# Who adds up the weight tiles of a seven-product gate matrix: GpSimd instead of VectorE

## The chip, the cores and the metric

The kernel runs on one core of one Trainium2 chip. The metric is the device time in microseconds (us) of one execution. The kernel before took 2365.54 us, the median of three runs (2364.66 to 2366.19). One more execution was recorded by the hardware profiler; all rows below are from it.

Engines are named as in the profile: PE is the matrix engine (PEld its loading of weights), DVE is VectorE, ACT is ScalarE, POOL is GpSimd, SP only issues transfers here. SBUF is the on-chip memory, a bank is an accumulator of PE.

## The reference

Two transformer layers over 512 positions of 1024 features, in float32: the first with two SwiGLU blocks around a mixer, the second with a mixer, a memory attention and a third SwiGLU block. What matters here is a SwiGLU block; there are three of them, of hidden width 2816.

```python
def swiglu_ffn(h, w_in, w_out):
    a, b = jnp.split(h @ w_in, 2, axis=-1)
    return (jax.nn.silu(a) * b) @ w_out

def _swiglu(h, w_gate, w_up, w_down):
    return (jax.nn.silu(h @ w_gate) * (h @ w_up)) @ w_down
```

## The kernel before, in words

All matrix products are made of float32 operands that are split in two parts, `hi` and `lo`, each of which PE takes whole: a product is `hi*hi + hi*lo + lo*hi`, three matmuls. Activations are split once and kept; weights are streamed. A *unit* is one weight tile of 128 rows and up to 1024 columns. It goes through four hands: SP issues its load into one of four `raw` buffers, ACT writes `whi` (one of three buffers; L1747), DVE writes `raw - whi` over the raw data as `wlo` (L2206), and PE multiplies. A `raw` buffer is loaded again when PE is through with the unit of four before, and `whi` is written again when PE is through with the unit of three before.

All engines walk through the same list of work items; each program is written out in this order, and within an engine nothing overtakes. Before the item that uses unit u, ACT and DVE put the splits of the units up to u+2.

In the second and third SwiGLU block most products with the gate matrix are not made directly. Two neighbouring tiles of 128 gate columns and two blocks of 128 rows form a 2 by 2 block matrix, whose product with a 2 by 2 block of the activations takes seven block products in place of eight (a Strassen scheme in Winograd's form). The sums of the activations are made once. The sums of the weights are made for each unit: it is loaded with four tiles of 128x128, and four more are added up from them in place, so that the unit is 1024 columns wide again. This is `add_up`: one instruction for two tiles (L2340) and one each for the other two (L2343, L2345), of which each needs the one before. ACT may split the unit only when the last sum is there (the semaphore `w_sum`). There are 60 such units in 15 *rounds*. A round makes two gate tiles and the two tiles of the other matrix that belong to them:

- unit q0 (seven block products, 21 matmuls of 256 columns), then b (a plain unit, 24 matmuls of 512 columns), q1
- `ffg` of the odd tile of the round before: DVE takes its bank (L2334), multiplies (L2396), ACT copies, DVE writes the low half (L2211)
- `ffv`: DVE takes b's bank (L2334, `t_bt`)
- q2, q3, then `ffm`: ACT copies out a quarter (`t_p`), DVE joins the seven products by six instructions on the banks (L2366 to L2373) and two more (L2377)
- b2 (plain), and `ffg` of the even tile

The rounds use six banks: four for q0 to q3, one each for b and b2. The next round's q0 takes the same four, and so waits until the last of the six instructions (L2373) has read them.

The rounds stand in four stretches: 3 and 5 rounds in the second block (from 1122 to 1191 us and from 1258 to 1354 us of the span), 2 and 5 in the third (2058 to 2104 and 2172 to 2267 us). In a stretch a prime marks the units of the next round: q0', b' and so on.

In DVE's program the sums stand between the splits: as far as the unit after the one just split, and up to three units ahead of the item:

```python
while n < min(upto - 1 + NHI, len(unit)):
    while a < min(n + 1 + (n in summands), upto + NHI, len(unit)):
        if a in summands:
            add_up(a)
        a += 1
    split(n)
    n += 1
```

Of the kernel before, what the change touches and what calls it, by code (L numbers as in the profile page):

```python
# [10 lines left out]
ALU = mybir.AluOpType  # L11
# [3 lines left out]
P = 128  # L15
# [72 lines left out]
NHI = 3  # L88
WARM = 6
NRAW = 4  # L90
# [889 lines left out]
def build(nc, A, out):  # L980
    stack = ExitStack()
    w = order()
    unit = w.units
# [12 lines left out]
    def place(name, at, cols, dt=F32):  # L996

        assert at + cols <= ARENA + NRAW * UNIT
        return nc.alloc_sbuf_tensor_at("t_" + name, [P, cols], dt, offset=base + 4 * at)[:]

    def f32(ap):
        return ap.bitcast(F32)

    raw = [place(f"raw{i}", ARENA + i * UNIT, UNIT) for i in range(NRAW)]
# [109 lines left out]
    def spare(hd, t):  # L1114

        return (pp2 if hd.kind in ("win", "mm2") else pp)[t % RING]
# [10 lines left out]
    def width(hd, i):  # L1127
        if hd.kind == "spa":
            return (i + 1) * P
        return P if hd.kind == "win" and i == 0 else 256  # L1130
# [11 lines left out]
    def signal(name):  # L1142
        return Signal(stack.enter_context(nc.semaphore("s_" + name)))

    full = signal("bank_full")
    w_hi, w_lo, w_sum, x_full = signal("weight_hi"), signal("weight_lo"), signal("weight_sum"), signal("operand_full")
# [4 lines left out]
    d_raw = [signal(f"d_raw{i}") for i in range(NRAW)]  # L1151
# [16 lines left out]
    def squares(what, h, q):  # L1168
        if what == "k":
            return T[h][:, 256 * q:256 * q + 256]  # L1170
        return T[q] if h else T[2 + q]
# [1018 lines left out]
    summands = set(w.seven)  # L2190

    def dve_program(e):
        on = Once(e)
# [3 lines left out]
        def split(n):  # L2197
            name, _, width, _ = unit[n]
            width = UNIT if n in summands else width
            on.wait_ge(*w_hi.at(n))  # L2200
            if name in STACKED:
                m, at = STACKED[name]
                x, hi = (t.rearrange("p (k c) -> p k c", k=KD) for t in (raw[n % NRAW], whi[n % NHI]))
                e.tensor_tensor(hi[:, :, at:at + m], x[:, :, 0:m], f32(hi[:, :, 0:m]), ALU.subtract).then_inc(*w_lo.tick(n))
                return
            e.tensor_tensor(wlo[n % NRAW][:, 0:width], raw[n % NRAW][:, 0:width], f32(whi[n % NHI][:, 0:width]),  # L2206
                            ALU.subtract).then_inc(*w_lo.tick(n))
# [125 lines left out]
            on.wait_ge(*full.at(item))  # L2333
            e.tensor_tensor(o, banks[item], RB, ALU.mult).then_inc(*evac.tick(done, ("free", item)))  # L2334

        def add_up(n):
            r = raw[n % NRAW]
            on.wait_ge(*d_raw[n % NRAW].at(n))
            two = r[:, 512:768].rearrange("p (a c) -> p a c", a=2)
            e.tensor_tensor(two, r[:, 128:384].rearrange("p (a c) -> p a c", a=2), r[:, 384:512].unsqueeze(1).to_broadcast([P, 2, P]),  # L2340
                            ALU.add).then_inc(*w_sum.tick(("two", n)))
            on.wait_ge(*w_sum.at(("two", n)))
            e.tensor_tensor(r[:, 768:896], r[:, 640:768], r[:, 128:256], ALU.add).then_inc(*w_sum.tick(("three", n)))  # L2343
            on.wait_ge(*w_sum.at(("three", n)))
            e.tensor_tensor(r[:, 896:1024], r[:, 768:896], r[:, 0:128], ALU.add).then_inc(*w_sum.tick(n))  # L2345

        def xna(f, j):
            b, a = TN[j % 2]
            x = NS[j]
            on.wait_ge(*x_full.at(("xn", f, j)))  # L2350
            e.tensor_tensor(x[:, 0:256], b[:, 256:512], b[:, 0:256], ALU.subtract).then_inc(*calc.tick(("xn1", f, j)))
            e.tensor_tensor(x[:, 256:512], b[:, 256:512], a[:, 256:512], ALU.subtract).then_inc(*calc.tick(("xn3", f, j)))
            on.wait_ge(*calc.at(("xn1", f, j)))
            e.tensor_tensor(x[:, 512:768], a[:, 256:512], x[:, 0:256], ALU.subtract).then_inc(*calc.tick(("xn2", f, j)))
            on.wait_ge(*calc.at(("xn2", f, j)))
            e.tensor_tensor(x[:, 768:1024], a[:, 0:256], x[:, 512:768], ALU.subtract).then_inc(*calc.tick(("xns", f, j)))
# [544 lines left out]
        def final(k):  # L2901
            n = 2 if k < 6 else 1
            if k == 7:
# [13 lines left out]
                  winzero=winzero, kaz=kaz, vaf=vaf, vas=vas, qa=qa, oasum=oasum, oa=oa, om=om, alr=alr, gq=gq, gkv=gkv, gdec=gdec, gone=gone, glog=glog, gcum=gcum, ggate=ggate,  # L2917
                  gkt=gkt, gstate=gstate, gg=gg, gsq=gsq, gnorm=gnorm, gfin=gfin, osplit=osplit, mk2s=mk2s, mk2d=mk2d,
                  mem2zero=mem2zero, mv2s=mv2s, mq2x=mq2x, mq2s=mq2s, mmo=mmo, final=final)
        n, a = 2, 2  # L2920
        for (kind, *args), upto in w.items:
            while n < min(upto - 1 + NHI, len(unit)):
                while a < min(n + 1 + (n in summands), upto + NHI, len(unit)):
                    if a in summands:
                        add_up(a)
                    a += 1
                split(n)
                n += 1
            while a < min(upto + NHI, len(unit)):
                if a in summands:  # L2930
                    add_up(a)
                a += 1
            if kind in do:
                do[kind](*args)

    def pool_program(e):
        on = Once(e)

        def scale(t):
            hd, i = w.tiles[t]  # L2940
            wd = width(hd, i)
            p, r = spare(hd, t)[:, 0:wd], sa[t % RING][:, 4:5]
            on.wait_ge(*calc.at(("rc", t)))
            if hd.kind == "spa":
                on.wait_ge(*calc.at(("gn",)))
                k = 3 * (4 * hd.more["g"] + hd.more["r"]) + 1 + hd.more["a"]
                e.tensor_scalar(p, p, r, gn[:, i, k:k + 1], ALU.mult, ALU.mult).then_inc(*scaled.tick(t))  # L2947
            else:
                on.wait_ge(*d_c.at(0))
                e.tensor_scalar(p, p, r, cst[:, C_ONE:C_ONE + 1], ALU.mult, ALU.mult).then_inc(*scaled.tick(t))  # L2950

        def widestat(what, h):
            a, b = squares(what, h, 0), squares(what, h, 1)
            on.wait_ge(*curve.at(("wsq", what, h, 1)))
            e.tensor_tensor(a, a, b, ALU.add).then_inc(*summed.tick(("wsq", what, h)))

        def winload():
            on.wait_ge(*full.at(("ffo", 1, 0, 0)))
            e.memset(lrw, 0.0).then_inc(*cleared.tick("lrw"))

        def hidzero():
            on.wait_ge(*full.at(("memv", 1, 1)))
            for q in range(2):
                e.memset(hk[2 * q], 0.0)
                e.memset(hk[2 * q + 1], 0.0).then_inc(*cleared.tick("hid"))

        def cclear(g):
            on.wait_ge(*full.at(("values", 3 + 8 * g)))
            for q in range(2):
                e.memset(f32(PCT[q]), 0.0).then_inc(*cleared.tick(("kcp", g)))  # L2970

        def final(k):
            if k == 7:
                on.wait_ge(*curve.at(("gain", 7)))
                on.wait_ge(*copied.at(("rb", 6)))
                e.tensor_tensor(XT[:, 7, :], XT[:, 7, :], RB, ALU.mult).then_inc(*scaled.tick(("final", 7)))

        do = dict(widestat=widestat, winload=winload, final=final, cclear=cclear, scale=scale, hidzero=hidzero)
        for (kind, *args), _ in w.items:
            if kind in do:  # L2980
                do[kind](*args)

# [89 lines left out]
    for program in (pe_program, act_program, dve_program, pool_program, sp_program):  # L3072
        program(Count())
# [3 lines left out]
    block.tensor(pe_program)  # L3077
    block.scalar(act_program)
    block.vector(dve_program)
    block.gpsimd(pool_program)  # L3080
    block.sync(sp_program)
    stack.close()
# [80 lines left out]
```

## Time and profile before

| | |
|---|---|
| median of three runs | 2365.54 us |
| the profiled execution | 2364.08 us |
| its span, first to last instruction | 2362.3 us |
| clock granted to PE | 0.999 of full speed |
| PE busy | 2338.0 us (99%) |
| DVE busy | 1559.0 us (66%) |
| ACT busy | 1051.7 us (45%) |
| POOL busy | 165.5 us (7%) |
| DMA, mean over the span | 98 GB/s |

A matmul's record is longer than its share of the engine: matmuls are pipelined, and of 512 columns one starts every 0.227 us though each is shown with 0.39 us, of 256 columns one every 0.120 us with 0.28 us. PE's small stops are therefore read from the distance of starts. A row of a timeline gives start, duration, engine, line, operation, tiles and shapes, the count of merged instructions, and in brackets the idle time before it and what ended it. The chain that ended last runs over PE for 96% of the span.

### The profile page before, as it was taken

To read this page: it belongs to the slowest core of one execution; us is meant where nothing else is said; L and a number is where in the kernel's file an instruction comes from. 1 tells how busy PE (TensorE), PEld (TensorE's weight loads), DVE (VectorE), ACT (ScalarE), POOL (GpSimd) and SP (SyncE) were. 2 spreads that over 40 slices of the span, in tenths; PEclk is the share of its full clock that TensorE was granted. 3 is DMA by queue.
4 is the path that set the end of the run, shared out by engine and by line. 5 is a ranking of instruction groups with operands and counts; after the bars stand their busy time and mean duration, and the time that the engine had idled before them with its cause. 6 is when DMAs were issued, how large, how long until landed. Compare 5 with 4: busy or idle time off the path is not lost.

```text
span 2362.3 us, 31755 instructions
## 1 busy us (share of the span) xinstructions
PE 2338.0 (99%) x11988; PEld 1980.8 (84%) x11988; DVE 1559.0 (66%) x3231; ACT 1051.7 (45%) x1921; POOL 165.5 (7%) x250
## 2 busy tenths in 40 slices
PE   9999999999999999999999999999999999999998
PEld 7888889888888888878888888888888887888887
DVE  6434546674757897877756856677754667774864
ACT  4323335432335676664333434666523346432432
POOL 0000000110001222310000000111100001000000
PEclk9999999999999999999999999999999999999999
DMA  4454434332322211122233333211123332233232
GB/s 151 118 117 144 118 109 153 111 109 84 116 94 86 77 54 63 59 92 96 90 104 103 98 117 120 81 54 55 63 89 114 123 112 72 90 97 95 94 106 90
DMA packets 98416, 231.42 MB, mean 98 GB/s; under 512 B 8984, under 2 KB 39320, under 8 KB 98266
## 3 DMA queue, kind: packets, MB, share of 16 engines
q1 hardware_dynamic: 93072, 221.42, 28.3%
q10 hardware_dynamic: 5194, 7.98, 2.1%
q8 instruction: 97, 1.59, 0.3%
q14 instruction: 53, 0.43, 0.1%
HBM read 217.83 MB, written 11.53 MB: 97 GB/s over the span
## 4 chain that ended last, share of the span: by engine, by line
PE 96%; DVE 2%; ACT 1%; issue 1%; DMA 0%; POOL 0%; DVEq 0%; SPq 0%; ACTq 0%
PE bank L1186 93%; PE bank L1453 2%; PE bank L1261 1%; PE bank L1627 0%; PE bank L1282 0%; DVE t_pw L2532 0%; DMA t_XT<-in_xT 0%; DVE t_pp L2532 0%; DVE t_PS L2211 0%; DVE t_wlo L2206 0%; DVE t_XL L2215 0%; ACT t_whi L1747 0%; ACT t_pw L1917 0%; DVE t_XT L2908 0%; POOL t_pw L2950 0%
## 5 line engine op out<-in xcount | busy, mean ns | idle before, releaser
L1186 PE MATMUL bank<-t_XH,t_whi 128*128 128x512 f32 (+1 forms) x2004 | 770.4, 384 | 1.2 <-DVE t_wlo L2206 0.5
L1186 PE MATMUL bank<-t_XL,t_whi 128*128 128x512 f32 (+1 forms) x2004 | 761.6, 380 | 0.0
L1186 PE MATMUL bank<-t_XH,t_wlo 128*128 128x512 f32 (+1 forms) x1988 | 755.5, 380 | 0.0
L2206 DVE TENSOR_TENSOR t_wlo<-t_raw,t_whi 128x1024 fp32r<-128x1024 f32 (+2 forms) x446 | 514.2, 1156 | 322.3 <-ACT t_whi L1747 318.5
L1747 ACT ACTIVATE t_whi<-t_raw 128x1024 fp32r<-128x1024 f32 (+3 forms) x452 | 448.3, 993 | 427.4 <-PE bank L1186 320.0
L1186 PEld LDWEIGHTS bank<-t_XH,t_whi 128*128 128x128 f32 x2004 | 377.1, 188 | 75.6 <-DVE t_tmp L2373 2.6
L1186 PEld LDWEIGHTS bank<-t_XH,t_wlo 128*128 128x128 f32 x1988 | 373.8, 188 | 72.0
L1186 PEld LDWEIGHTS bank<-t_XL,t_whi 128*128 128x128 f32 x2004 | 377.4, 188 | 67.5
L1186 PE MATMUL bank<-t_RX,t_whi 128*128 128x512 f32 x1056 | 325.2, 389 | 0.0
L1186 PEld LDWEIGHTS bank<-t_RX,t_whi 128*128 128x128 f32 x1056 | 198.3, 188 | 40.9
L1186 PE MATMUL bank<-t_RX,t_wlo 128*128 128x512 f32 x528 | 205.4, 389 | 0.0
L2334 DVE TENSOR_TENSOR t_tmp<-bank,t_RB 128x512 f32<-128x512 f32 x133 | 91.6, 689 | 104.3 <-PE bank L1186 95.5
L1186 PEld LDWEIGHTS bank<-t_RX,t_wlo 128*128 128x128 f32 x528 | 99.1, 188 | 20.7
L2947 POOL TENSOR_SCALAR t_pp<-t_pp,t_sa,t_gn 128x512 f32<-128x512 f32 (+3 forms) x128 | 88.7, 699 | 334.9 <-DVE t_sa L2545 334.4
L1747 ACT ACTIVATE t_RX<-t_tmp 128x512 fp32r<-128x512 f32 x66 | 41.7, 632 | 156.9 <-DVE t_tmp L2396 156.9
L1917 ACT ACTIVATE t_pp<-t_pp,t_sa 128x256 f32<-128x256 f32 (+3 forms) x144 | 79.6, 554 | 53.1 <-DVE t_sa L2532 52.3
L2950 POOL TENSOR_SCALAR t_pw<-t_pw,t_sa,t_cst 128x256 f32<-128x256 f32 (+1 forms) x80 | 47.9, 604 | 722.2 <-DVE t_sa L2545 692.8
L1852 ACT ACTIVATE t_tmp<-t_tmp 128x512 f32<-128x512 f32 x66 | 41.5, 629 | 126.8 <-DVE t_tmp L2334 85.8
L1747 ACT ACTIVATE t_XH<-t_XT,t_vec 128x512 fp32r<-128x512 f32 x48 | 34.5, 723 | 109.2 <-DVE t_XT L2409 52.6
L1186 PE MATMUL bank<-t_OA,t_whi 128*128 128x512 f32 x256 | 79.4, 391 | 0.0
L2409 DVE SCALAR_TENSOR_TENSOR t_XT<-bank,t_XT 128x512 f32<-128x512 f32 x47 | 32.5, 691 | 68.6 <-PE bank L1186 68.6
L2211 DVE TENSOR_TENSOR t_RX<-t_tmp,t_RX 128x512 fp32r<-128x512 f32 x66 | 45.8, 693 | 46.0 <-ACT t_RX L1747 46.0
(360 smaller groups left out, 3197.5 us busy)
## 6 DMA issues: line engine op xcount, KB each, us to landing
t_raw<-in_f_in SPq DMA_DIRECT2D x70, 512.0 KB, 3.2
t_raw<-in_f_out SPq DMA_DIRECT2D x32, 384.0 KB, 3.1
t_raw<-in_w_conv SPq DMA_DIRECT2D x24, 512.0 KB, 3.2
t_raw<-in_w_merge SPq DMA_DIRECT2D x24, 512.0 KB, 3.2
t_raw<-in_fu SPq DMA_DIRECT2D x22, 512.0 KB, 3.2
t_raw<-in_f_out SPq DMA_DIRECT2D x32, 320.0 KB, 2.9
t_raw<-in_f_in SPq DMA_DIRECT2D x36, 256.0 KB, 2.8
t_raw<-in_w_g SPq DMA_DIRECT2D x16, 512.0 KB, 3.2
```

The source lines that it names most:

```text
L1186: return e.matmul(o, l, r, start=start, stop=stop, skip_group_check=True)
L1261: f = e.transpose(b[:, i * P:(i + 1) * P], r, ident)
L1453: f = e.transpose(b[:, j * P:(j + 1) * P], spare(hd, t)[:, j * P:(j + 1) * P], ident)
L1747: return e.activation(o, i, ACT.Copy, **how)
L1852: e.activation(s, a, ACT.Silu).then_inc(*curve.tick(("silu", f, h, m)))
L1917: e.activation(p, p, ACT.Exp, scale=-1.0, bias=s[:, 0:1], accum_out=s[:, 1:2]).then_inc(*curve.tick(("ex", t)))
L2206: e.tensor_tensor(wlo[n % NRAW][:, 0:width], raw[n % NRAW][:, 0:width], f32(whi[n % NHI][:, 0:width]), ALU.subtract).then_inc(*w_lo.tick(n))
L2211: e.tensor_tensor(o, x, f32(hi), ALU.subtract).then_inc(*x_lo.tick(item, *more))
L2334: e.tensor_tensor(o, banks[item], RB, ALU.mult).then_inc(*evac.tick(done, ("free", item)))
L2409: e.scalar_tensor_tensor(XT[:, m, :], banks[item], HALF[f], XT[:, m, :], ALU.mult, ALU.add).then_inc(*evac.tick(("free", item), *done))
L2947: e.tensor_scalar(p, p, r, gn[:, i, k:k + 1], ALU.mult, ALU.mult).then_inc(*scaled.tick(t))
L2950: e.tensor_scalar(p, p, r, cst[:, C_ONE:C_ONE + 1], ALU.mult, ALU.mult).then_inc(*scaled.tick(t))
```

## The change

`add_up` moves from DVE's program into POOL's, as it stands. DVE's loop keeps only the splits. POOL's loop, which so far took only items of its own, puts before each item the sums of units up to three beyond the item's own (`upto + NHI`). The waits are the same: on the unit's load, on the sum before, and ACT's on `w_sum`.

```diff
@@ dve_program
-        def add_up(n):
-            r = raw[n % NRAW]
-            on.wait_ge(*d_raw[n % NRAW].at(n))
-            two = r[:, 512:768].rearrange("p (a c) -> p a c", a=2)
-            e.tensor_tensor(two, r[:, 128:384].rearrange("p (a c) -> p a c", a=2), r[:, 384:512].unsqueeze(1).to_broadcast([P, 2, P]),
-                            ALU.add).then_inc(*w_sum.tick(("two", n)))
-            on.wait_ge(*w_sum.at(("two", n)))
-            e.tensor_tensor(r[:, 768:896], r[:, 640:768], r[:, 128:256], ALU.add).then_inc(*w_sum.tick(("three", n)))
-            on.wait_ge(*w_sum.at(("three", n)))
-            e.tensor_tensor(r[:, 896:1024], r[:, 768:896], r[:, 0:128], ALU.add).then_inc(*w_sum.tick(n))
...
-        n, a = 2, 2
+        n = 2
         for (kind, *args), upto in w.items:
             while n < min(upto - 1 + NHI, len(unit)):
-                while a < min(n + 1 + (n in summands), upto + NHI, len(unit)):
-                    if a in summands:
-                        add_up(a)
-                    a += 1
                 split(n)
                 n += 1
-            while a < min(upto + NHI, len(unit)):
-                if a in summands:
-                    add_up(a)
-                a += 1
             if kind in do:
                 do[kind](*args)
@@ pool_program
+        def add_up(n):
...
         do = dict(widestat=widestat, winload=winload, final=final, cclear=cclear, scale=scale, hidzero=hidzero)
-        for (kind, *args), _ in w.items:
+        n = 2
+        for (kind, *args), upto in w.items:
+            while n < min(upto + NHI, len(unit)):
+                if n in summands:
+                    add_up(n)
+                n += 1
             if kind in do:
                 do[kind](*args)
```

On DVE, from `ffv` of one round to `ffm`: before, the sum of q0' (three rows on `t_raw`) stands between the splits of b2 and of q0'.

```order
L2334 TENSOR_TENSOR t_bt_182<-bank,t_RB 128x512 [waits s_bank_full]
L2206 TENSOR_TENSOR t_wlo_55<-t_raw_51,t_whi 128x1024 [waits s_weight_hi]
L2340 TENSOR_TENSOR t_raw_52<-t_raw_52 128x256 [waits s_d_raw3]
L2343 TENSOR_TENSOR t_raw_52<-t_raw_52 128x128 [waits s_weight_sum]
L2345 TENSOR_TENSOR t_raw_52<-t_raw_52 128x128 [waits s_weight_sum]
L2206 TENSOR_TENSOR t_wlo_56<-t_raw_52,t_whi 128x1024 [waits s_weight_hi]
L2366 TENSOR_TENSOR t_p_185<-bank,t_p_184 128x256 [waits s_bank_copied]
```

And now, at the same place (line numbers from here on are smaller by 11 in the changed kernel):

```order
L2334 TENSOR_TENSOR t_bt_182<-bank,t_RB 128x512 [waits s_bank_full]
L2206 TENSOR_TENSOR t_wlo_55<-t_raw_51,t_whi 128x1024 [waits s_weight_hi]
L2206 TENSOR_TENSOR t_wlo_56<-t_raw_52,t_whi 128x1024 [waits s_weight_hi]
L2355 TENSOR_TENSOR t_p_185<-bank,t_p_184 128x256 [waits s_bank_copied]
```

The three rows are gone; the two splits and `ffm` follow each other. The other three sums of a round go in the same way: that of q1' from ahead of L2396, those of q2' and q3' from around the split of q1'.

On POOL, in the same round: before, nothing stands there (the memset of `t_lrw`, whose wait ends between the first two stretches, is followed by work of the second mixer). Now:

```order
L2963 TENSOR_TENSOR t_raw_52<-t_raw_52 128x256 [waits s_d_raw3]
L2966 TENSOR_TENSOR t_raw_52<-t_raw_52 128x128 [waits s_weight_sum]
L2968 TENSOR_TENSOR t_raw_52<-t_raw_52 128x128 [waits s_weight_sum]
L2963 TENSOR_TENSOR t_raw_50<-t_raw_50 128x256 [waits s_d_raw1]
L2966 TENSOR_TENSOR t_raw_50<-t_raw_50 128x128 [waits s_weight_sum]
L2968 TENSOR_TENSOR t_raw_50<-t_raw_50 128x128 [waits s_weight_sum]
```

These are the sums of q0' (buffer 52) and q1' (buffer 50), one unit after another, with no other wait than that for the load and for the sum before.

## Rows read from the trace of the kernel before

**Rows 1.** The page, busy time of each engine, share of the span, instructions.

```profile
PE 2338.0 (99%) x11988; PEld 1980.8 (84%) x11988; DVE 1559.0 (66%) x3231; ACT 1051.7 (45%) x1921; POOL 165.5 (7%) x250
```

**Rows 2.** Busy time in the four stretches of rounds, summed (us; x instructions).

```profile
sum 306.00, PE 305.74 PEld 273.53 DVE 242.45 ACT 120.89 POOL 0.00; mean PE 76.44 PEld 68.38 DVE 60.61 ACT 30.22 POOL 0.00
```

**Rows 3.** Timeline of PE where a round begins, in four rounds; 1332.58 is q1'.

```profile
1180.01 0.39 PE L1186 MATMUL bank<-t_XH,t_wlo 128*128 128x512 f32 x1
1180.33 0.36 PE L1186 MATMUL bank<-t_XH,t_whi 128*128 128x256 f32 x1
...
1324.19 0.39 PE L1186 MATMUL bank<-t_XH,t_wlo 128*128 128x512 f32 x1
1324.52 0.36 PE L1186 MATMUL bank<-t_XH,t_whi 128*128 128x256 f32 x1
...
1332.58 0.28 PE L1186 MATMUL bank<-t_XH,t_whi 128*128 128x256 f32 x1
...
2213.49 0.39 PE L1186 MATMUL bank<-t_XH,t_wlo 128*128 128x512 f32 x1
2214.14 0.36 PE L1186 MATMUL bank<-t_XH,t_whi 128*128 128x256 f32 x1 [0.26 <-issue]
...
2256.16 0.39 PE L1186 MATMUL bank<-t_XH,t_wlo 128*128 128x512 f32 x1
2256.48 0.36 PE L1186 MATMUL bank<-t_XH,t_whi 128*128 128x256 f32 x1
```

**Rows 4.** Timeline of DVE, one round of the second stretch.

```profile
1317.22 1.22 DVE L2206 TENSOR_TENSOR t_wlo<-t_raw,t_whi 128x1024 fp32r<-128x1024 f32 x1
1318.35 0.42 DVE L2340 TENSOR_TENSOR t_raw<-t_raw 128x256 f32<-128x256 f32 x1
...
1320.55 1.23 DVE L2206 TENSOR_TENSOR t_wlo<-t_raw,t_whi 128x1024 fp32r<-128x1024 f32 x1 [1.13 <-ACT t_whi L1747]
...
1323.48 0.68 DVE L2373 TENSOR_TENSOR t_tmp<-bank,t_p 128x512 f32<-128x512 f32 x1
...
1338.39 1.22 DVE L2206 TENSOR_TENSOR t_wlo<-t_raw,t_whi 128x1024 fp32r<-128x1024 f32 x1
```

**Rows 5.** Timeline of ACT, the same round.

```profile
1319.45 1.06 ACT L1747 ACTIVATE t_whi<-t_raw 128x1024 fp32r<-128x1024 f32 x1 [2.53 <-DVE t_raw L2345]
...
1332.83 1.06 ACT L1747 ACTIVATE t_whi<-t_raw 128x1024 fp32r<-128x1024 f32 x1 [1.28 <-PE bank L1186]
```

**Rows 6.** Timeline of SP's issues, the same round.

```profile
1314.11 0.37 SPq L2997 DMA_DIRECT2D t_raw<-in_f_in  x1
...
1319.15 8.52 SPq L2997 DMA_DIRECT2D t_raw<-in_f_in  x3
```

**Rows 7.** The 60 loads of such units (L2997): issue to landing.

```profile
DMA to landing us min/median/max: 2.5/2.7/4.0
```

**Rows 8.** Groups on POOL by shape: count | busy us, mean ns | idle before, releasers.

```profile
L2955 POOL TENSOR_TENSOR t_tmp<-t_tmp 128x512 f32<-128x512 f32 x4 | 5.2, 1294 | 18.7 <-ACT t_tmp L1880 18.7
L2955 POOL TENSOR_TENSOR t_tmp<-t_tmp 128x256 f32<-128x256 f32 x4 | 3.0, 744 | 383.6 <-ACT t_tmp L1880 383.6
L2950 POOL TENSOR_SCALAR t_pw<-t_pw,t_sa,t_cst 128x128 f32<-128x128 f32 x16 | 7.3, 458 | 307.9 <-DVE t_sa L2545 301.1 <-DVE t_sa L2542 6.8
```

**Rows 9.** POOL's L2950 of 128x256: count, ns min/median/max, first and last start.

```profile
L2950 POOL TENSOR_SCALAR t_pp<-t_pp,t_sa,t_cst x16: 557/560/2501, 417.6 to 602.1; 128x256 f32<-128x256 f32 x16
```

**Rows 10.** Timeline of POOL at two places where DVE splits weights.

```profile
453.57 1.28 POOL L2955 TENSOR_TENSOR t_tmp<-t_tmp 128x512 f32<-128x512 f32 x1
...
495.03 2.50 POOL L2950 TENSOR_SCALAR t_pp<-t_pp,t_sa,t_cst 128x256 f32<-128x256 f32 x1 [9.33 <-DVE t_sa L2545]
```

**Rows 11.** Timeline of DVE at the same two places.

```profile
453.73 3.33 DVE L2206 TENSOR_TENSOR t_wlo<-t_raw,t_whi 128x1024 fp32r<-128x1024 f32 x2 [0.47 <-ACT t_whi L1747]
...
494.77 0.15 DVE L2545 RECIPROCAL t_sa<-t_sa 128x1 f32<-128x1 f32 x1
494.84 2.34 DVE L2206 TENSOR_TENSOR t_wlo<-t_raw,t_whi 128x1024 fp32r<-128x1024 f32 x2
```

More of the change, by code:

```diff
@@ L2976, in final @@
                 e.tensor_tensor(XT[:, 7, :], XT[:, 7, :], RB, ALU.mult).then_inc(*scaled.tick(("final", 7)))
-        do = dict(widestat=widestat, winload=winload, final=final, cclear=cclear, scale=scale, hidzero=hidzero)
-        for (kind, *args), _ in w.items:
+        def add_up(n):
+            r = raw[n % NRAW]
+            on.wait_ge(*d_raw[n % NRAW].at(n))
+            two = r[:, 512:768].rearrange("p (a c) -> p a c", a=2)
+            e.tensor_tensor(two, r[:, 128:384].rearrange("p (a c) -> p a c", a=2), r[:, 384:512].unsqueeze(1).to_broadcast([P, 2, P]),
+                            ALU.add).then_inc(*w_sum.tick(("two", n)))
+            on.wait_ge(*w_sum.at(("two", n)))
+            e.tensor_tensor(r[:, 768:896], r[:, 640:768], r[:, 128:256], ALU.add).then_inc(*w_sum.tick(("three", n)))
+            on.wait_ge(*w_sum.at(("three", n)))
+            e.tensor_tensor(r[:, 896:1024], r[:, 768:896], r[:, 0:128], ALU.add).then_inc(*w_sum.tick(n))
+        do = dict(widestat=widestat, winload=winload, final=final, cclear=cclear, scale=scale, hidzero=hidzero)
+        n = 2
[4 more added lines that the diff above has]
+                n += 1
             if kind in do:
```

## The prediction

> **What bounds the kernel now.** I read the page first. PE is busy for 2338.0 of 2362.3 us [rows 1], so a gain is at most what PE's stops hold, and a loss is whatever makes PE stop. The change touches only the four stretches of rounds, so I read these next: summed over them, PE is busy 305.74 of 306.00 us, DVE 242.45, ACT 120.89 and POOL 0.00 [rows 2]. DVE is at work four fifths of the time, but nobody there waits for DVE as a whole; what counts is which wait on its chain ends last.
>
> The busy time hides PE's small stops, since a matmul's record overlaps the next one's. By the distance of starts there is one where a round's q0 begins: after the last matmul of b2, at 1324.19, the next starts 0.33 us later, where 0.227 is usual, and is itself shown with 0.36 in place of 0.28 us, so some 0.17 to 0.18 us are lost [rows 3]. I find this at seven of the 15 q0, the first at 1180.33 and the last at 2256.48; six are of this size, the one at 2214.14 is 0.65 − 0.23 + 0.07, about 0.5 us [rows 3]. In all 6 × 0.17 + 0.5 = 1.5 us. Elsewhere in the stretches no start is late by 0.1 us.
>
> What ends that stop is the bank: the last instruction of `ffm` on the banks, L2373, starts at 1323.48 and takes 0.68, to 1324.16, and q0's first matmul follows 0.36 later at 1324.52 [rows 3, 4]. Behind it stands a chain on DVE and ACT: split of b2 at 1317.22, sum of q0' from 1318.35, ACT's split of q0' at 1319.45, DVE's at 1320.55, then `ffm` [rows 4, 5]. So in the later rounds of a stretch the sum is on the chain that PE waits for, and 0.1 us more there is 0.1 us more of PE. The next tight place is b2: its split ends 1338.39 + 1.22 = 1339.61; with the 0.36 us from write to matmul that is 1339.97. PE goes on from b' at 1332.58 with three q units of 21 × 0.12 = 2.52 us and wants b2 near 1340.1: 0.15 us of slack [rows 3, 4].
>
> **The change part by part.** Taken from DVE: 60 sums. The first instruction is 0.42 us, and from its start at 1318.35 to ACT's at 1319.45 a whole sum is 1.1 us [rows 4, 5]. That is 66 us less of DVE and by itself nothing for PE, except where the sum stands on the chain above.
>
> Added to POOL: 60 × 3 instructions. POOL's add of two SBUF tiles takes 0.744 us for 256 columns and 1.294 for 512 [rows 8], 2.15 ns a column; for 128 columns I estimate 0.744 − 128 × 2.15 ns = 0.47. A tensor_scalar of 128 columns, 0.458 [rows 8], is the lower bound, the 256-column add, 0.744, the upper. The first instruction reads one operand three-dimensionally, once broadcast, which no row shows on POOL: bounds 0.744 and, for twice the columns, 1.294; I take 0.744, the same column count. From a DVE result to POOL's start 0.11 us pass (494.77 + 0.15 to 495.03) [rows 10, 11]; I take 0.1 for each of the two inner waits. A free sum is then 0.744 + 2 × 0.47 + 0.2 = 1.9 us, 0.8 more than on DVE (by the upper bounds 1.294 + 2 × 0.744 + 0.2 = 3.0). In return it need not stand in DVE's row: it starts when the load lands. The order of loads and splits, and PE's program, are unchanged; no new DMA, and the only new wait is POOL's for the load, behind which nothing but other sums is queued in these stretches.
>
> The sums are not free, though. POOL's add of 453.57 (1.28 us, to 454.85) runs beside two splits of DVE that take 3.33 us in place of 2.34 [rows 10, 11]: the first is held until POOL is done and ends about 1.1 us later. In the other direction a 0.56 us instruction of POOL takes 2.50 us at 495.03, until two splits that stand back to back (494.84 to 497.18) are over [rows 9, 10, 11]. So a DVE instruction with two SBUF inputs and an instruction of POOL exclude each other, and DVE's back-to-back instructions keep POOL out. The Trainium skill has the first half of this (SBUF — State Buffer, section Who interferes with whom): a VectorE instruction with two SBUF inputs contends with a GpSimd instruction that reads SBUF, one fully blocks. The trace agrees, with 3.33 us against 2.34. Were it otherwise, the sums would run freely and the result would be the first rival below; with it, the splits, L2396, L2377 and L2211 of DVE all stand against the sums.
>
> Now one round, placed by hand. *Place A, the sum of q0'.* Issue 1314.11, landing 2.7 us later at 1316.8 [rows 6, 7], some 1.5 us before DVE took it up. POOL's first instruction runs 1316.9 to 1317.65. DVE's split of b2, ready at 1317.22, is held and ends near 1318.75 in place of 1318.44: 0.3 late. POOL's second instruction is held in turn by this split, and runs to about 1319.15, the third to 1319.7; ACT starts near 1319.75 in place of 1319.45. So the early start is lost in full, and the chain to the banks is 0.3 us later. *Place B, the sums of q2' and q3'.* The last of the three loads is issued at 1319.15 + 8.52 − 0.37 = 1327.30 [rows 6] and lands at 1330.0. POOL has q2' in hand from 1327.4 on: 1.9 us, and in the way L2211 (0.69) and the split of q1' (1.22), so it comes to 1330.5 to 1331.2. Then q3': 1.9 us and the split of q2' (1.13), to 1333.5 to 1334.2, where ACT took it at 1332.83 as soon as PE let it [rows 5]. That is 0.7 to 1.4 late if every collision happens. But DVE's instructions there come up to 2 us earlier (three sums have left its row), so that some fall ahead of a landing; I take 0 to 0.5. What is late here reaches b2, through L2334, L2396, ACT's copy and the split at 1338.39, where 0.15 us are free.
>
> A and B lie on one chain through the round. I take 0.3 us a round: place A in full, place B hidden by the earlier row on DVE. Bounds: −0.17 (no collision, the stop goes) and +0.8 (0.3 + 0.5). There are 15 − 4 = 11 passages from one round to the next within a stretch: 11 × 0.3 = 3.3 us. I count the four that have no stop now like the others, since the chain is within a few tenths there. The profiled execution took 2364.08 us, 1.8 of it outside the span; it would take 2367.4. The median of the runs stands 1.5 above it, at 2365.54, and goes to 2368.8 us. What a measurement of this kernel can tell from no change is about 0.2%, 4.7 us: below 2360.8 or above 2370.3.
>
> **The rivals.** *The stops vanish.* If the sums fall mostly between DVE's instructions, the chain gets 1.1 us shorter and PE's 1.5 us are gained: 2364.0. For it: POOL is idle in all four stretches, loads land 1.5 us ahead. Against: the split of b2 is ready 0.3 us after POOL's first start, in every round. It can't be faster by more, since PE has no other stops there.
>
> *The collisions add up (slower).* Place B decides: if the sum of q3' is ready over 0.5 us after PE frees ACT's buffer, b2's split is late as well and each round loses 0.8: 11 × 0.8 = 8.8 us, 2374.3. For it: POOL kept out for 2.50 us by back-to-back splits [rows 10]. Against: between the splits of q1' and q2' DVE waits for ACT.
>
> *POOL's adds are dear.* With the upper bounds a sum is 1.1 us longer, q2' and q3' stand behind each other, so 2.2 + 0.3 us a round, 11 × 2.5 = 27 us, 2393. Against: only the broadcast form is unknown.
>
> That the change doesn't do what it says is excluded by the order: the three rows are gone from DVE and stand on POOL.
>
> **How the numbers follow.** Forecast 0.50, stops vanish 0.22, collisions add up 0.20, dear adds 0.08. Forecast's own range 2365.5 to 2372 (0 to 0.6 a round); about a sixth of it, 0.08, is above 2370.3. Slower: 0.08 + 0.20 + 0.08 = 0.36; faster 0.02, for something unseen; same 0.62. The range 2363.5 to 2377 holds the first rival, the forecast and the second rival (with 1.0 a round), and leaves out the dear adds and the tails.
>
> **What would show it.** Right: POOL's three instructions at some 0.75, 0.47 and 0.47 us where nothing is in the way, longer where a split runs; splits of up to 1.9 us on DVE; PE's stop ahead of q0 at 0.4 to 0.5 us rather than 0.17, and hardly one ahead of b2. DVE about 60 us less busy, POOL 100 us or more busier. Wrong: no stop at q0 (the first rival), stops ahead of b2 in each round (the second), or POOL's first instruction at over 1 us with DVE idle beside it (the third).

## The result and the profile after

| | before | after |
|---|---|---|
| median of the runs | 2364.91 us (2363.36 to 2366.54, 22 runs) | 2368.72 us (2366.54 to 2370.46, 22 runs) |
| ratio after : before | | 1.0015, 95% interval 1.0009 to 1.0021 |
| the profiled execution | 2364.08 us | 2368.48 us |
| its span | 2362.3 us | 2366.6 us |

The changed kernel is slower by 3.8 us of 2365 (2.1 to 5.0 by the interval): a loss, though one of less than the 0.2% within which I had called it no change.

The page, busy time of each engine after:

```profile
PE 2340.9 (99%) x11988; PEld 1983.5 (84%) x11988; DVE 1510.2 (64%) x3051; ACT 1050.6 (44%) x1921; POOL 303.3 (13%) x430
```

Against [rows 1], 180 instructions went from DVE to POOL. DVE lost 48.8 us of busy time, POOL got 137.8. The three groups of the new instructions, by shape (count | busy us, mean ns of one | idle before, and what ended it):

```profile
L2963 POOL TENSOR_TENSOR t_raw<-t_raw 128x256 f32<-128x256 f32 x60 | 49.2, 820 | 442.8 <-DMA t_raw<-in_f_in 226.6 <-DMA t_raw<-in_fg 216.1
...
L2968 POOL TENSOR_TENSOR t_raw<-t_raw 128x128 f32<-128x128 f32 x60 | 48.5, 809 | 4.7
L2966 POOL TENSOR_TENSOR t_raw<-t_raw 128x128 f32<-128x128 f32 x60 | 41.6, 694 | 4.7
```

In all 139.3 us. What one of them takes with nothing in its way, and what with a split of DVE in its way, is read in the timeline. POOL, one round (the same round of the program as in [rows 3 to 6], some 2.3 us later on the clock); the first three rows are the sum of q0', then q1', q2' and q3':

```profile
1319.11 0.73 POOL L2963 TENSOR_TENSOR t_raw<-t_raw 128x256 f32<-128x256 f32 x1 [5.30 <-DMA t_raw<-in_f_in]
1319.93 1.32 POOL L2966 TENSOR_TENSOR t_raw<-t_raw 128x128 f32<-128x128 f32 x1
1321.32 0.46 POOL L2968 TENSOR_TENSOR t_raw<-t_raw 128x128 f32<-128x128 f32 x1
1323.97 0.76 POOL L2963 TENSOR_TENSOR t_raw<-t_raw 128x256 f32<-128x256 f32 x1 [2.19 <-DMA t_raw<-in_f_in]
1324.81 0.47 POOL L2966 TENSOR_TENSOR t_raw<-t_raw 128x128 f32<-128x128 f32 x1
1325.35 0.46 POOL L2968 TENSOR_TENSOR t_raw<-t_raw 128x128 f32<-128x128 f32 x1
1329.70 0.74 POOL L2963 TENSOR_TENSOR t_raw<-t_raw 128x256 f32<-128x256 f32 x1 [3.89 <-DMA t_raw<-in_f_in]
1330.52 0.79 POOL L2966 TENSOR_TENSOR t_raw<-t_raw 128x128 f32<-128x128 f32 x1
1331.39 1.32 POOL L2968 TENSOR_TENSOR t_raw<-t_raw 128x128 f32<-128x128 f32 x1
1332.68 0.74 POOL L2963 TENSOR_TENSOR t_raw<-t_raw 128x256 f32<-128x256 f32 x1
1333.50 0.46 POOL L2966 TENSOR_TENSOR t_raw<-t_raw 128x128 f32<-128x128 f32 x1
1334.04 1.35 POOL L2968 TENSOR_TENSOR t_raw<-t_raw 128x128 f32<-128x128 f32 x1
```

DVE in the same round: the split of b2, the split of q0', the release of the banks (the old L2373), the splits of q1' and q2', and the split of b2':

```profile
1319.40 1.53 DVE L2206 TENSOR_TENSOR t_wlo<-t_raw,t_whi 128x1024 fp32r<-128x1024 f32 x1
1322.91 1.23 DVE L2206 TENSOR_TENSOR t_wlo<-t_raw,t_whi 128x1024 fp32r<-128x1024 f32 x1 [1.98 <-ACT t_whi L1747]
...
1325.84 0.68 DVE L2362 TENSOR_TENSOR t_tmp<-bank,t_p 128x512 f32<-128x512 f32 x1
...
1331.11 1.29 DVE L2206 TENSOR_TENSOR t_wlo<-t_raw,t_whi 128x1024 fp32r<-128x1024 f32 x1
1333.84 1.22 DVE L2206 TENSOR_TENSOR t_wlo<-t_raw,t_whi 128x1024 fp32r<-128x1024 f32 x1 [1.44 <-ACT t_whi L1747]
...
1340.97 1.22 DVE L2206 TENSOR_TENSOR t_wlo<-t_raw,t_whi 128x1024 fp32r<-128x1024 f32 x1
```

The two lists are to be read side by side. Free adds (q1') take 0.76, 0.47 and 0.46 us. Where a split stands in the way, an add takes 1.3 us and ends just after the split: 1319.93 + 1.32 = 1321.25 beside the split that ends at 1320.93, and so at 1331.39 and 1334.04. In the other direction the split of b2 takes 1.53 instead of 1.22, since POOL's first add runs until 1319.84. Over all, POOL pays more: 139.3 us against 60 × (0.74 + 0.47 + 0.46) = 100, so 39 us of holding. DVE lost 48.8 us of busy time, though its sums took 60 (60 × (0.42 + 0.29 + 0.29)); most of the difference is that a sum's record overlaps the one before it (1318.35 lies ahead of 1317.22 + 1.22 in [rows 4]). What DVE was held for is read from its groups with two SBUF inputs: the splits took 431.2 us in place of 428.9, the low halves of `ffg` (L2211) 46.9 in place of 45.8, the two multiplications of `ffm` (L2377) 19.9 in place of 19.2, some 4 us in all.

Where it comes back to PE. ACT's waits in the second stretch, 1258 to 1366 us (what waited <- for what: us in total, times, longest), first before:

```profile
ACT t_whi L1747 <- DVE t_raw L2345: 18.3, 10, 2.8
...
ACT t_whi L1747 <- PE bank L1186: 11.9, 6, 3.0
```

and after:

```profile
ACT t_whi L1747 <- POOL t_raw L2968: 34.7, 15, 4.3
...
ACT t_whi L1747 <- PE bank L1186: 2.0, 1, 2.0
```

Before, six of ACT's splits in this stretch started as soon as PE freed the buffer; after, one. The others now wait for POOL's last add. PE's own rows, after, at a b2, at a q0 and at the last b2 of the second stretch (start, duration):

```profile
1320.86 0.28 PE L1186 MATMUL bank<-t_XH,t_wlo 128*128 128x256 f32 x1
1321.08 0.47 PE L1186 MATMUL bank<-t_XH,t_whi 128*128 128x512 f32 x1
...
1326.37 0.39 PE L1186 MATMUL bank<-t_XH,t_wlo 128*128 128x512 f32 x1
1326.88 0.36 PE L1186 MATMUL bank<-t_XH,t_whi 128*128 128x256 f32 x1
...
1363.63 0.28 PE L1186 MATMUL bank<-t_XH,t_wlo 128*128 128x256 f32 x1
1364.89 0.47 PE L1186 MATMUL bank<-t_XH,t_whi 128*128 128x512 f32 x1 [0.98 <-DVE t_wlo L2206]
```

A stop is read as for [rows 3]: the distance of starts above 0.12 or 0.227 us, plus what the next distance has too much (0.07 to 0.08). At 1321.08 it is 0.17 us, at 1326.88 0.36, at 1364.89 1.22. POOL and DVE ahead of the last of these three:

```profile
1352.41 1.79 POOL L2963 TENSOR_TENSOR t_raw<-t_raw 128x256 f32<-128x256 f32 x1 [4.92 <-DMA t_raw<-in_f_in]
```

```profile
1352.38 1.23 DVE L2206 TENSOR_TENSOR t_wlo<-t_raw,t_whi 128x1024 fp32r<-128x1024 f32 x1 [0.26 <-ACT t_whi L1747]
```

I added up all stops in the rounds, by place, for every kernel that was run (the last b2 of a stretch, which lies behind the windows of [rows 2], is counted with it). The kernels with e are the experiments below; each difference is to the kernel before of the same series, 2364.80 us for e1, e2, e3 and e4, 2365.76 us for the others:

| kernel | stops ahead of q0, us (count) | ahead of b2, us (count) | together, less before | measured: difference of medians, us; ratio (95%) |
|---|---|---|---|---|
| before | 1.51 (7) | 0.15 (1) | | |
| after | 2.18 (7) | 2.62 (6) | +3.1 | +3.8; 1.0015 (1.0009 to 1.0021) |
| e1_writes | 0 | 0 | −1.7 | −0.7; 0.9995 (0.9986 to 1.0004) |
| e2_q0_dve | 3.10 (7) | 2.62 (5) | +4.1 | +4.9; 1.0019 (1.0011 to 1.0028) |
| e3_q0_pool | 2.82 (8) | 0.62 (4) | +1.8 | +2.7; 1.0011 (1.0003 to 1.0020) |
| e3b_q1_pool | 1.65 (7) | 0 | 0.0 | −0.3; 0.9998 (0.9989 to 1.0007) |
| e4_fourth | 5.72 (8) | 11.43 (11) | +15.5 | +17.6; 1.0069 (1.0056 to 1.0083) |
| e5_beside | 3.31 (7), and 0.78 (3) ahead of q1 | 2.37 (5) | +4.8 | +5.9; 1.0025 (1.0016 to 1.0034) |
| e6b_after_early | 0 | 2.14 (9) | +0.5 | +0.8; 1.0003 (0.9994 to 1.0011) |
| e7b_before_early | 0 | 0 | −1.7 | −1.6; 0.9993 (0.9985 to 1.0002) |

The two columns at the right agree to about 1 us, less than the interval of a ratio leaves open (0.0009 is 2 us); for e4, of five runs only, to 2.1 us where the interval leaves 3. So PE's stops at these places carry the result, and of the 3.1 us lost by the change 2.47 (2.62 − 0.15) stand ahead of b2 and 0.67 ahead of q0. Where a stop stands is not yet what made it: e2 and e3 below show that each place makes stops at the other, too.

### The profile page after: what moved, and what is told of

The parts are those of the page before. It is cut to its first block, busy times and chain, and to the rows that moved or that the text cites. A ratio compares the mean times of both kernels' runs of the same rounds, so it can differ in the third digit from the quotient of the medians.

```text
span 2366.6 us, 31755 instructions
## 1 busy us (share of the span) xinstructions
PE 2340.9 (99%) x11988; PEld 1983.5 (84%) x11988; DVE 1510.2 (64%) x3051; ACT 1050.6 (44%) x1921; POOL 303.3 (13%) x430
## 4 chain that ended last, share of the span: by engine, by line
PE 95%; DVE 2%; ACT 1%; issue 1%; DMA 1%; POOL 0%; SPq 0%; DVEq 0%; ACTq 0%
PE bank L1186 91%; PE bank L1453 2%; PE bank L1261 1%; DVE t_wlo L2206 0%; PE bank L1627 0%; ACT t_whi L1747 0%; PE bank L1282 0%; DMA t_XT<-in_xT 0%; DVE t_pw L2521 0%; DMA t_raw<-in_f_in 0%; DVE t_PS L2211 0%; DMA t_raw<-in_fg 0%; POOL t_raw L2963 0%; ACT t_pw L1917 0%; DVE t_XT L2897 0%
## 5 line engine op out<-in xcount | busy, mean ns | idle before, releaser
L2963 POOL TENSOR_TENSOR t_raw<-t_raw 128x256 f32<-128x256 f32 x60 | 49.2, 820 | 442.8 <-DMA t_raw<-in_f_in 226.6
```

## The experiments

The theory: a POOL add that reads SBUF and a DVE instruction with two SBUF inputs exclude each other; the loss is made where a sum meets a split on the chain to PE (place A, the sum of q0'; place B, those of q2' and q3').

**Reads or writes.** Rival: GpSimd is slow to start and to signal, and the longer sum by itself is the loss.

```diff
...
+            e.memset(r[:, 512:1024], 0.0).then_inc(*w_sum.tick(("two", n)))
             on.wait_ge(*w_sum.at(("two", n)))
-            e.tensor_tensor(r[:, 768:896], r[:, 640:768], r[:, 128:256], ALU.add).then_inc(*w_sum.tick(("three", n)))
+            e.memset(r[:, 512:1024], 0.0).then_inc(*w_sum.tick(("three", n)))
...
```

> The changed kernel with GpSimd's three adds replaced by three memsets of 512 columns each at the same place and with the same waits (the sums are left out, the output is not the reference's). A memset reads nothing from SBUF; three take about as long as the three adds do alone (3 x 0.53 = 1.6 us against 1.7). Theory (VectorE's instructions with two SBUF inputs and GpSimd's reads exclude each other): no split is held and no memset is stretched, the unit is ready about 1.9 us after its load lands, which is earlier than VectorE's sum was; the stops of PE ahead of q0 (0.36 us in the changed kernel, 0.17 before) and of b2 go, so 1.5 us less than before, ratio 0.9993. Rival (GpSimd is late because its instructions and semaphores are slow, whatever VectorE does): stops as in the changed kernel, ratio 1.0015.

POOL in the same round, a unit that DVE's split of b2 meets; then that split:

```profile
1318.78 0.53 POOL L2962 MEMSET t_raw<- 128x512 f32 x1 [6.15 <-DMA t_raw<-in_f_in]
1319.36 0.53 POOL L2964 MEMSET t_raw<- 128x512 f32 x1
1319.94 0.52 POOL L2966 MEMSET t_raw<- 128x512 f32 x1
```

```profile
1319.21 1.21 DVE L2206 TENSOR_TENSOR t_wlo<-t_raw,t_whi 128x1024 fp32r<-128x1024 f32 x1
```

The split lies over three instructions of POOL and takes its 1.21 us; POOL's take theirs. So it is in all rounds: no memset takes over 0.53 us, no split over 1.23. The unit is ready 1.68 us after POOL's start, and ACT's split of q0', which waits for POOL's last memset as it waits for the last add in the changed kernel, starts at 1320.50, 1.29 us after the split of b2 began, where it was 2.23 us before [rows 4, 5]; the 0.2 us that a free sum takes longer would fit in. Every stop of PE in the rounds is gone. So neither POOL's signals nor its slower work cost PE anything: what costs is that POOL reads SBUF beside DVE. The rival falls.

**Place B without place A.** Only the sum of q0' goes back to DVE; q1' to q3' stay on POOL. (In e2, e3 and e3b the sums stand in both programs, and a set says which units of a round POOL adds up; they differ in this set alone.)

```diff
+    on_pool = {n for n in w.seven if unit[n][1][1] in (1, 2, 3)}
```

> The sums of q0 back on VectorE, those of q1, q2, q3 on GpSimd. Theory, place A (the sum of q0 is on the chain to the banks, 0.3 us a round): the stop ahead of q0 returns to about 0.17 us; what is left is the lateness of q2 and q3 (0.17 us ahead of b2 in some rounds), so 0 to +1.5 us, ratio 1.0000 to 1.0006. Rival (place B, the pair q2 and q3, makes the loss): stops ahead of both as in the changed kernel, ratio 1.0013 or more.

Here my theory that place A makes the loss fell: 1.0019, not less than the changed kernel. ACT's splits of q2' and q3' wait for POOL, and b2 is late:

```profile
1334.25 1.06 ACT L1748 ACTIVATE t_whi<-t_raw 128x1024 fp32r<-128x1024 f32 x1 [2.35 <-POOL t_raw L2989]
1336.92 1.06 ACT L1748 ACTIVATE t_whi<-t_raw 128x1024 fp32r<-128x1024 f32 x1 [1.61 <-POOL t_raw L2989]
```

The stops ahead of q0 double to 3.10 us although the sum of q0' stands on DVE again. DVE's split of b2 and its release of the banks:

```profile
1320.41 1.21 DVE L2208 TENSOR_TENSOR t_wlo<-t_raw,t_whi 128x1024 fp32r<-128x1024 f32 x1
...
1326.67 0.68 DVE L2375 TENSOR_TENSOR t_tmp<-bank,t_p 128x512 f32<-128x512 f32 x1
```

The chain to the banks is as long as before: from the split of b2 at 1320.41 to the end of the release at 1327.35 it is 6.94 us, as from 1317.22 to 1324.16 [rows 4]. But it begins with b2's split, and that is now late. Lateness made at B is paid at b2 and again at the next q0.

**Place A alone.**

```diff
+    on_pool = {n for n in w.seven if unit[n][1][1] in (0,)}
```

> Only the sums of q0 on GpSimd, the others on VectorE as before. Theory, place A: q0's second add is held by the split of b2, the stop ahead of q0 grows to about 0.36 us in the later rounds of each stretch, no stop ahead of b2; +2 us, ratio 1.0008 (1.0004 to 1.0013). Rival (place B makes the loss): as before, ratio 1.0000.

1.0011, which fits a cost at place A: it costs too. The four stops ahead of b2 (0.62 us) I had not expected: at three of them DVE's split of b2 is itself held by POOL's first add and takes 1.65 to 1.70 us. Both places are real, and they don't add up: +1.8 and +4.1 us of stops alone, +3.1 together. With q0' on POOL as well, its sum doesn't wait behind the late split of b2; that this returns a part of what B costs is my reading, which no run tests by itself.

**A sum that meets nothing.** q1' was the one that POOL made freely in the round above.

```diff
+    on_pool = {n for n in w.seven if unit[n][1][1] in (1,)}
```

> The kernel before with the sum of q1' alone on GpSimd, the one of the four that ran on GpSimd without being held. Theory (a sum costs where it meets a split on the chain; q1' has over 2 us before ScalarE wants it): ratio 1.0000, 0.9996 to 1.0004, stops as in the kernel before (0.17 ahead of q0, none ahead of b2). Rival (any sum on GpSimd costs by its length): 1.0005 and more, with new stops.

POOL in the same round:

```profile
1321.90 0.74 POOL L2984 TENSOR_TENSOR t_raw<-t_raw 128x256 f32<-128x256 f32 x1 [19.31 <-DMA t_raw<-in_f_in]
1322.71 0.46 POOL L2987 TENSOR_TENSOR t_raw<-t_raw 128x128 f32<-128x128 f32 x1
1323.26 0.46 POOL L2989 TENSOR_TENSOR t_raw<-t_raw 128x128 f32<-128x128 f32 x1
```

While POOL reads here, DVE is at `ffm` (from 1321.59 on), which takes one operand from a bank, and neither holds the other. No loss and no gain, 0.9998; PE's stop ahead of q0 is 0.17 us in most rounds, as before.

**More of the same.** The last add of each sum made twice on POOL.

```diff
+            e.tensor_tensor(r[:, 896:1024], r[:, 768:896], r[:, 0:128], ALU.add).then_inc(*w_sum.tick(("four", n)))
+            on.wait_ge(*w_sum.at(("four", n)))
```

> The changed kernel with the last sum made twice by GpSimd (same values), a fourth dependent instruction per unit. Theory (the sums are on the chain that PE waits for, and each dependent add gives VectorE one more turn): 0.55 us more for q0 and 0.55 to 1.7 more for q2 and q3 together, so stops ahead of q0 of 0.8 to 1 us or stops ahead of b2 as well; +0.6 to +1.2 us in each of 11 passages over the changed kernel, ratio to before 1.0043 to 1.007. Rival (the sums have slack, the loss comes from elsewhere, such as VectorE being held): ratio as in the changed kernel, 1.0015 to 1.002.

1.0069: one more add of 0.46 us a sum, and the loss grows more than fourfold, with two thirds of the stops ahead of b2 (11.43 of 17.2 us). The rival, that the sums have slack, falls; each add lengthens the chain and is one more that can be held. The stops at the two places explain 15.5 of the 17.6 us; the rest is within the interval, 3 us on either side.

**Holding without waiting.** The kernel before, and in the third block alone POOL adds constants beside the sums that DVE makes; nobody waits for them.

```diff
+        def beside(n):
...
+            on.wait_ge(*d_raw[n % NRAW].at(n))
...
+            e.tensor_tensor(scr, cst[:, 0:256], cst[:, 0:256], ALU.add).then_inc(*w_psum.tick(("two", n)))
...
+            e.tensor_tensor(scr[:, 0:128], cst[:, 0:128], cst[:, 128:256], ALU.add).then_inc(*w_psum.tick(("three", n)))
...
+            e.tensor_tensor(scr[:, 0:128], cst[:, 0:128], cst[:, 128:256], ALU.add).then_inc(*w_psum.tick(("last", n)))
```

> The kernel before, VectorE makes all sums; in the rounds of the third block alone (7 of 15, 5 passages) GpSimd makes three adds of the same sizes from constants into a scratch tile whenever such a unit has landed, and nobody waits for them. Theory (GpSimd's adds cost by holding VectorE's instructions with two SBUF inputs): the split of b2 or the sum of q0' is held by 0.3 to 0.8 us at each passage, so 5 x 0.3 to 0.8 = 1.5 to 4 us, ratio 1.0006 to 1.0017, in the trace larger stops ahead of q0 or b2 in stretches 3 and 4 alone, splits of 1.5 us and more there, and the stops of stretches 1 and 2 as in the kernel before. Rival (the cost comes from ScalarE waiting for GpSimd's slower sums, and the holding is small): 1.0000, 0.9996 to 1.0003, stops of stretches 3 and 4 as before.

1.0025, above the range of my theory, and in the other direction from the rival. POOL in one of these rounds, then DVE's sum of q0' beside it, then PE at that q0:

```profile
2232.64 1.49 POOL L2988 TENSOR_TENSOR t_scr<-t_cst 128x128 f32<-128x128 f32 x1
2234.21 0.52 POOL L2990 TENSOR_TENSOR t_scr<-t_cst 128x128 f32<-128x128 f32 x1
```

```profile
2233.74 0.68 DVE L2342 TENSOR_TENSOR t_raw<-t_raw 128x256 f32<-128x256 f32 x1
2234.45 0.43 DVE L2345 TENSOR_TENSOR t_raw<-t_raw 128x128 f32<-128x128 f32 x1
2234.92 0.29 DVE L2347 TENSOR_TENSOR t_raw<-t_raw 128x128 f32<-128x128 f32 x1
```

```profile
2239.27 0.39 PE L1188 MATMUL bank<-t_XH,t_wlo 128*128 128x512 f32 x1
2240.31 0.35 PE L1188 MATMUL bank<-t_XH,t_whi 128*128 128x256 f32 x1 [0.65 <-DVE t_tmp L2375]
```

DVE's own sum takes 0.4 us longer (0.68 and 0.43 in place of 0.42 and 0.29), and with b2 late by the same cause the stop at q0 becomes 0.89 us (1.04 − 0.23 + 0.08). The stops in the first two stretches are as before, four of 0.17. I had looked for long splits; only three of the 1024-column splits in the rounds took over 1.3 us, and what was held are mostly DVE's sums, which take 12.0 us more in all (29.4, 21.9 and 20.9 us by line in place of 25.2, 17.5 and 17.5). No instruction waits for POOL here, so holding alone is enough. A round loses more than in the changed kernel; I take it that this is because DVE is held and still has its sums to make.

**Another order, with and without the change.** The copy and the six bank instructions of `ffm` go ahead of the split of q0' on ACT and DVE; the two multiplications, `ffr` in the diff, stay behind it. The changed bound of the loop keeps the split of q0' from being put one item earlier.

```diff
         for (kind, *args), upto in w.items:
-            while n < min(upto - 1 + NHI, len(unit)):
+            if kind == "ffm":
+                do[kind](*args)
+            while n < min(upto - 1 + NHI - (kind == "ffs" and args[3] == 3), len(unit)):
...
+            if kind == "ffm":
+                ffr(*args)
+            elif kind in do:
                 do[kind](*args)
```

> The kernel before, with the copy and the six bank instructions of ffm put ahead of the split of q0' on ScalarE and VectorE (the two multiplications of ffm stay behind it). The banks are then free about 2 us earlier (near 1322.1 in place of 1324.16), and q0's split ends near 1323.3. Theory (the chain to the banks ends PE's stop ahead of q0): the seven stops are gone, 1.5 us less, ratio 0.9994, 0.9989 to 1.0000. Rival (q0's weights are then as late as the banks were): stops of some 0.2 us stay, 1.0000, 0.9997 to 1.0004.

> The changed kernel with the same two groups exchanged. Theory (place A acts through the release of the banks, place B, the sums of q2' and q3' kept out by VectorE's splits, through b2's split): the stops ahead of q0 are gone, those ahead of b2 (0.15 to 0.4) stay, so some 2 us of loss stay of 3.8: ratio 1.0004 to 1.0010. Rival 1 (all of it is place A's lateness handed on along the round): b2's stops go too, ratio 0.9994 to 1.0002. Rival 2 (the q0' chain ends at the weights, not at the banks): stops ahead of q0 stay, ratio 1.0015 as the changed kernel.

The kernel before in this order, DVE's release of the banks and the split of q0' behind it, then PE at q0:

```profile
1322.00 0.68 DVE L2375 TENSOR_TENSOR t_tmp<-bank,t_p 128x512 f32<-128x512 f32 x1
1322.60 1.21 DVE L2208 TENSOR_TENSOR t_wlo<-t_raw,t_whi 128x1024 fp32r<-128x1024 f32 x1
```

```profile
1324.82 0.39 PE L1186 MATMUL bank<-t_XH,t_wlo 128*128 128x512 f32 x1
1325.05 0.28 PE L1186 MATMUL bank<-t_XH,t_whi 128*128 128x256 f32 x1
```

The banks are free 2.4 us ahead of q0 and the split is done 1.2 us ahead; the distance of starts is 0.23, no stop. With the change (e6b) the stops ahead of q0 are gone too, those ahead of b2 stay, for instance at 1319.30:

```profile
1319.05 0.28 PE L1186 MATMUL bank<-t_XH,t_wlo 128*128 128x256 f32 x1
1319.30 0.47 PE L1186 MATMUL bank<-t_XH,t_whi 128*128 128x512 f32 x1
```

The first came out as expected, 0.9993. The second, 1.0003, lies a hair below the range of my theory and above that of its first rival; here the stops decide: none ahead of q0, nine ahead of b2, as the theory has it. So the stops ahead of q0 come through the banks, and stops ahead of b2, 2.14 us, stay without them. They are not all the same collisions as in the changed kernel, for the new order makes others: the two multiplications of `ffm` now stand beside the adds of q1' and take 7.2 us longer in all. The reordered kernel before has the lowest ratio (2364.12 against 2365.76 us). All its stops are gone in the trace; the interval of its ratio, 0.9985 to 1.0002, just includes no gain.

## Why the prediction came out as it did

The time (2368.8 forecast, 2368.72 measured) and the direction are right, and so is the mechanism, that POOL and DVE hold each other and PE waits for it. But the loss is not where I put it: two terms were mis-sized against each other, and that their sum agrees is luck. I forecast 3.3 us at place A and nothing at B; 0.67 us came ahead of q0 and 2.47 ahead of b2. The start was off as well, 2365.54 us by three runs, 2364.91 by 22, so that a loss of 3.8 in place of 3.3 gave the same time.

- *Price of POOL's adds*: right. 0.744, 0.47 and 0.47 us forecast, 0.73 to 0.76, 0.47 and 0.46 measured when free, with 0.08 between them. The three-dimensional broadcast operand costs nothing extra; the third rival falls.
- *POOL and DVE exclude each other*: right, shown by e1 (only writes, nothing held) and e5 (nobody waits, still slower). The Trainium skill (SBUF — State Buffer, section Who interferes with whom) has also the limit that e1 shows: a VectorE instruction with two SBUF inputs does not contend with a GpSimd instruction that only writes SBUF. In e1 the stops vanish, as the first rival had it; it would have needed sums that meet nothing, and falls.
- *Place A, 0.3 us a round*: the mechanism is right, the term too large. Start of b2's split to ACT's start on q0' was 1319.45 − 1317.22 = 2.23 us [rows 4, 5] and is 1321.82 − 1319.40 = 2.42, 0.19 more, and the stop grows by as much, from 0.17 to 0.36. Not all seven did: summed over the stretches q0's stops grew by 0.67 us, where I had 11 × 0.3 = 3.3.
- *Place B hidden by the earlier row on DVE*: the step that failed. From q0's first matmul to ACT's split of q3' it was 1332.83 − 1324.52 = 8.31 us [rows 3, 5] and is 1335.41 − 1326.88 = 8.53 (too little to stop PE at that b2'). DVE's rows came earlier, but splits still met the adds of both units, one each (1331.11 and 1333.84, above). I read b2's lateness in the trace in every round but the first of each stretch: b2's split starts 0.12 to 1.52 us later after the start of q1 than before. The worst is the last round of the second stretch, where POOL's first add (1352.41, 1.79 us) came 0.03 us behind the split of q1' (1352.38). In sum 2.47 us ahead of b2, nearly four fifths of the loss. At five of the six stops the split of b2 takes its usual 1.21 to 1.23 us and only starts late; at the sixth, 1321.08, it is also held (1.53 us), which is place A's doing. The second rival had the right place, and too high a price: 0.8 a round.
- *The slack of b2, 0.15 us*: wrong, it is 0.37. I took the 0.36 us from the bank's release to the matmul for the weights as well. Where b2's weights are late, PE starts 0.15 us after the end of their split (1319.40 + 1.53 = 1320.93, matmul at 1321.08); before it started 0.52 after (1317.22 + 1.22 = 1318.44, matmul at 1318.95). In one round the kernel before had no slack: its b2 at 2208.20 starts 0.15 us late, which I overlooked when I wrote that no other start is late by 0.1 us. Had I used 0.37, I would have hidden place B with even more confidence; what failed was the lateness.
- *11 passages*: A's count. B acts in the last round of a stretch too, where it made the largest stop (1.22 us).
- *A and B on one chain*: right; the losses of e2 and e3 don't add up.
- *What would show it*: the q0 stops came to 0.19 to 0.36 (0.4 to 0.5 said), those ahead of b2 were not "hardly one" but six, and the longest split in the rounds took 1.57 us (1.9 said), since POOL is mostly the one that is held. DVE gave back 48.8 of 60 us, POOL's 137.8 are "100 or more".

Not all of the 4.4 us between the two profiled executions is the change: PE falls back by 1.5 us near 934 us of the span, ahead of the first sum, with matmuls at twice their usual distance for a moment. The granted clock is 0.50 there (934 to 936 us), that is 1.2 in place of 2.4 GHz; in the kernel before it is 1.00 at the same place. Just ahead of it two matmuls start 1.3 us apart, as they do in the kernel before. Such a dip stands near 1027 us in the traces of e1, e2 and e3, and near 942 in that of e5, which differs from the kernel before only from the third block on; so it does not belong to the change. The stops of the rounds give 3.1.

## What to carry to other kernels

Moving elementwise work from DVE to an idle POOL lowers DVE's busy time (here by 48.8 us) and can still lengthen the chain that PE waits for, when both read SBUF: count, for each moved instruction, which two-input DVE instruction will stand beside it, and how much slack the next consumer has. Look for the collision in every unit of a round and not only at the one that ends the stop today; what is paid at one place shows up again at the next. Where a stop is ended by a buffer's release, putting the release ahead of work that has slack can do more than moving work to another engine: here it removed every stop, though the time it gained is not clear of noise.

## What the runs showed of the hardware

- The engine that comes second waits for the end of the other's instruction: an add of 128 columns beside a split ended 0.3 us after the split (1321.25 against 1320.93), and an add that came 0.03 us behind a split took 1.79 us in place of 0.74. Here POOL lost 39 us in 180 adds and DVE some 4: a split of 1.22 us is the longer obstacle, an add of 0.46 the shorter.
- Weights reach PE sooner than a bank does: 0.15 us from the end of DVE's split to the matmul that waited for it, 0.36 us from the end of DVE's last reading of the bank to the matmul that waited for that.
- POOL's memset of 512 columns took 0.53 us, its add of 128 columns 0.46: a write alone is cheap on POOL, and held nothing (no split over 1.23 us in the rounds of e1).
